# Splitting the products of a weight block around the arrival of its residue (hybrid encoder with PEER, one core)

## The chip, the cores and the metric

One core of one Trainium2 chip. The metric is the device time of one execution in microseconds (us). The kernel before took 3535.6 us, the median of three runs (3535.57 to 3549.32).

## What is computed

Two layers (DEPTH 2) over 512 tokens of width 1024, all in float32:

```python
for l in range(DEPTH):
    h = x @ w_in[l]                                  # 1024 x IN_WIDTH
    ...                                              # three groups of attention heads -> mix
    x = layer_norm(DEEPNORM_ALPHA * x + mix, ln1_g[l], ln1_b[l])
    ffn = peer_ffn(x, peer_w_q[l], peer_sub_keys[l], peer_u[l], peer_v[l])
    x = layer_norm(DEEPNORM_ALPHA * x + ffn, ln2_g[l], ln2_b[l])

def chunk(xc):                                       # in peer_ffn, 128 tokens
    q = (xc @ w_q).reshape(c, PEER_HEADS, 2, PEER_HALF_DIM)
    sc = jnp.einsum('chpd,hpnd->chpn', q, sub_keys)
    top_s, top_i = lax.top_k(sc, kk)                 # 16 of 128, two halves
    ...                                              # 16 of the 256 sums -> experts, gates
    ue = jnp.take(u, experts, axis=0)
    ve = jnp.take(v, experts, axis=0)
    act = jax.nn.gelu(jnp.einsum('chkd,cd->chk', ue, xc), approximate=False)
    return jnp.einsum('chk,chkd->cd', gates * act, ve)
```

The change concerns `xc @ w_q` (the query stage) and the products of x with the experts' rows u (the U stage).

## The kernel before, in words

**Products in three parts.** TensorE works on values rounded to its own 32-bit format (F32R). To keep float32 accuracy an operand is split into a cast part ("hi") and a residue ("lo", the original less the cast), and a product is the sum of three: hi x hi, hi x lo, lo x hi. `product()` (L1449) issues these three, on L1451, L1452 and L1453. The tokens' operand t_hi, t_lo is made once per use, in eight chunks of 128 rows: ScalarE casts (`round_chunks`), VectorE subtracts (`rest_chunks`, L994), and TensorE waits chunk by chunk in `split_chunk` (L1471) where an operand is used for the first time.

**Blocks of weights.** After the attention each layer goes through ST_PER = 16 + 128 + 128 blocks of weights, 128 x 1024 values (512 KB) each: 16 query blocks, 128 U blocks (128 experts each), 128 V blocks. A block goes through a ring of two slots s = 0, 1:

- SyncE loads it into st_raw (`st_load`, L378, the DMA on L381), once the residue of the block two before it, in the same slot, is done (it waits on st_l[s]);
- ScalarE casts it to st_hi (`round_block`, L853, L857), once it has landed and TensorE has finished the block two before it (st_used); it then raises st_h;
- GpSimd computes the residue st_lo = st_raw - st_hi (`rest_block`, L605, L608), and raises st_l[s];
- TensorE runs `stationary()` (L1631): it waits on st_l[s], and then runs, for each of 8 chunks c, the three products of L1451 to L1453 into one PSUM bank, 24 in all, 512 columns wide in the query stage and 384 (tokens 128 to 511) in the U stage. The last one raises st_used.

**Query stage.** `query_pair()` (L1650) runs two blocks and then two sets of four products with the sub-keys; ScalarE copies the queries and the scores out (L875, L880). The first block of the first pair waits for t_lo chunk by chunk. Its residue is made by VectorE (L1000), the others by GpSimd.

**U stage.** `experts()` (L1660) waits until the gelu of the block two before it has emptied its PSUM bank and calls `stationary()`. On ScalarE the order is written out by hand: gelu of block b (L887, into h_out, which SyncE stores on L397), then the cast of block b + 2; before each pair an activation table is loaded. The first 88 U blocks (PRE = 44 pairs) run with nothing between them on TensorE. The other 40 lie between one-hot products of the gates (`spread`, L1684), a stage called B here, which needs the gates of all tokens first: an Exp on ScalarE, a few steps on VectorE (L1317 to L1321), then transposes on TensorE (L1674).

**Beside the 88 blocks.** The first 128 tokens take another way, by gathered rows. VectorE walks 24 units of the top-16 search (`unit`, L1207) in 12 rounds of two, and in each round 8 dot products of x with gathered rows of u (L1292, 512 KB each). A round ends with the eight dots stored (L1305). GpSimd issues the gathers (`gather_rows`, L617, L619) in the same queue in which it computes the residues, in an order written out by hand (`zone`, L635): eight gathers at first, six residues, then six zones of about two rounds, 12 residues and 16 gathers each. A gather waits until VectorE has used the slot's previous row.

**V stage.** Values are weighted and summed with `gather()`, which waits for the cast part and for the residue at separate points already.

Of the kernel before, what the change touches and what calls it, by code (L numbers as in the profile page):

```python
# [37 lines left out]
DC = D // P  # L38
# [31 lines left out]
ST_PER = QB + 2 * EB  # L70
# [63 lines left out]
def build(nc, a, out):  # L134
# [18 lines left out]
    t_hi = keep.tile("t_hi", [P, DC, T], F32R)  # L153
    t_lo = keep.tile("t_lo", [P, DC, T], F32R)
# [73 lines left out]
    st_hi = pr.tile("st_hi", [P, 2, DC, P], F32R)  # L228
    st_lo = pr.tile("st_lo", [P, 2, DC, P], F32R)
# [58 lines left out]
    def sem(name):  # L288
        return ctx.enter_context(nc.semaphore(name))
# [31 lines left out]
    st_h, st_used = sem("st_h"), sem("st_used")  # L321
    st_l = [sem(f"st_l{s}") for s in range(2)]
# [1116 lines left out]
    def _(pe):  # L1439
# [9 lines left out]
        def product(dst, lhs, rhs, first, last):  # L1449

            nc.tensor.matmul(dst, lhs[0], rhs[0], start=first, stop=False)  # L1451
            nc.tensor.matmul(dst, lhs[0], rhs[1], start=False, stop=False)  # L1452
            return nc.tensor.matmul(dst, lhs[1], rhs[0], start=False, stop=last)  # L1453

        with pe.Fori(0, L) as l:
# [15 lines left out]
            def split_chunk(u, c):  # L1471

                pe.wait_ge(tr_lo, DC * (3 * l + u) + c + 1)
# [31 lines left out]
            for k in range(3):  # L1505
                for tb in range(TB):
                    last = nc.tensor.transpose(ps[:, k, tb * P:(tb + 1) * P], lat_n[:, tb, k * P:(k + 1) * P], ident[:])
# [5 lines left out]
            for tb in range(TB):  # L1513
                bank = 4 * ((tb + 1) % 2)
                rows = slice(tb * P, (tb + 1) * P)
# [5 lines left out]
                for half in range(2):  # L1521
                    for k in range(2):
                        last = nc.tensor.matmul(ps[:, bank + half, 0:w], lat_t[:, k, rows],
                                                w_uq[:, k, half * w:(half + 1) * w], start=k == 0, stop=k == 1)
                last.then_inc(lat_ps, 1)
                w = UKV_W // 2
                for half in range(2):
                    last = nc.tensor.matmul(ps[:, bank + 2 + half, 0:w], lat_t[:, 2, rows],
                                            w_ukv[:, half * w:(half + 1) * w], start=True, stop=True)
# [100 lines left out]

            def stationary(m, s, dst, rows, operand=None):  # L1631

                pe.wait_ge(st_l[s], ST_PER // 2 * l + m + 1 + 1)
                for c in range(DC):
                    if operand is not None:
                        split_chunk(operand, c)
                    last = product(dst, (st_hi[:, s, c], st_lo[:, s, c]), (t_hi[:, c, rows], t_lo[:, c, rows]), c == 0,
                                   c == DC - 1)
                last.then_inc(st_used, 1)

            def key_scores(f, s):
# [8 lines left out]
            def query_pair(i, operand=None):  # L1650
                for s in range(2):
                    stationary(i, s, ps[:, s], slice(0, T), operand if s == 0 else None)
                for s in range(2):
                    key_scores(2 * i + s, s)
# [5 lines left out]
            def experts(m, s):  # L1660

                pe.wait_ge(gelu_done, EB * l + 2 * m + s + 1)
                stationary(m + QB // 2, s, ps[:, s, 0:TN], slice(P, T))
# [7 lines left out]
            for k in range(3):  # L1671
                src = e_all[:].rearrange("p u k -> p (u k)") if k == 2 else i_all[:, k]
                for d in range(DB):
                    last = nc.tensor.transpose(ps[:, SEL_BANKS[k], d * P:(d + 1) * P], src[:, (d + 1) * P:(d + 2) * P], ident[:])  # L1674
# [126 lines left out]
```

## Time and profile before

| what | value |
|---|---|
| median of three runs | 3535.6 us (3535.57 to 3549.32) |
| the profiled execution, its own time | 3530.59 us |
| its span, first to last instruction | 3529.0 us |
| TensorE products busy | 3294.9 us (93%) |
| TensorE weight loads busy | 2961.4 us (84%) |
| VectorE busy | 2491.6 us (71%) |
| ScalarE busy | 1367.2 us (39%) |
| GpSimd busy | 1956.2 us (55%) |
| mean granted TensorE clock | 0.977 of full speed |
| bytes moved | 765.11 MB, mean 217 GB/s |

The two layers look alike. In the first, attention runs to about 380 us, the query stage from 393 to 504, the first 88 U blocks to about 938, stage B to 1215, the V stage to 1760.

How to read the rows below. PE is TensorE's products, PEld its weight loads, DVE VectorE, ACT ScalarE, POOL GpSimd, SPq SyncE's queue of DMA issues. A product's shown duration includes its way through the array, so that consecutive ones overlap; the distance between starts of weight loads tells their pace. "<-" behind a time in brackets names what ended the idle time before the instruction, and that time is the number ahead of it.

### The profile page before, as it was taken

The numbers are of one execution on the slowest core, as the hardware profiler recorded it, in microseconds if no ns is written. First come the engines' busy times: TensorE is split into PE (matmuls) and PEld (weight loads), VectorE is DVE, ScalarE is ACT, GpSimd is POOL, SyncE is SP. The second block draws the span as 40 slices with busy tenths as digits, with TensorE's granted clock in tenths as the row PEclk, the third lists the DMA queues.
The fourth block names the chain that finished last, engine by engine and source line by source line (L and its number), as shares of the span: only waits on it lengthen the run. The fifth ranks groups of instructions, "written<-read, shape, count | busy, mean of one in ns | idle before, by whom it ended". The sixth has DMA issues, their size and how long they took to land.

```text
span 3529.0 us, 67255 instructions
## 1 busy us (share of the span) xinstructions
PE 3294.9 (93%) x18452; PEld 2961.4 (84%) x18454; DVE 2491.6 (71%) x5419; ACT 1367.2 (39%) x2110; POOL 1956.2 (55%) x1558
## 2 busy tenths in 40 slices
PE   8999898889999899999899998989899998999996
PEld 8888788888999788888688887888889988888885
DVE  1454554888787688898924545458887877889898
ACT  2354244444433333333324542444444333333332
POOL 3434346777654266666544342467776543666664
PEclk9999999999999999999999999999999999999998
DMA  4001137888788599999820011378887985999996
GB/s 159 25 1 60 48 103 230 285 283 287 248 257 260 161 335 323 338 339 337 306 86 25 1 60 54 111 233 287 282 284 248 270 251 169 347 337 337 339 336 231
DMA packets 402485, 765.11 MB, mean 217 GB/s; under 512 B 162400, under 2 KB 261472, under 8 KB 398432
## 3 DMA queue, kind: packets, MB, share of 16 engines
q1 hardware_dynamic: 197088, 462.06, 39.0%
q0 software_dynamic: 73728, 268.47, 20.8%
q10 hardware_dynamic: 131584, 33.56, 4.5%
q8 instruction: 40, 0.66, 0.1%
q14 instruction: 45, 0.37, 0.0%
HBM read 677.98 MB, written 85.98 MB: 216 GB/s over the span
## 4 chain that ended last, share of the span: by engine, by line
PE 55%; issue 21%; POOL 11%; DVE 5%; DMA 3%; ACTq 3%; ACT 1%; POOLq 1%; DVEq 1%; SPq 0%
PE ps L1717 24%; POOL st_lo L608 6%; PE ps L1451 6%; PE ps L1452 6%; PE ps L1453 6%; PE ps L1684 4%; PE ps L1573 3%; POOL u_row L619 3%; PE ps L1550 3%; ACTq L934 2%; PE ps L1558 2%; DMA h_in<-gelu_d 2%; PE ps L1539 1%; DMA st_raw<-in_peer_v 1%; DMA u_row<-in_peer_ur,idx_u 1%
## 5 line engine op out<-in xcount | busy, mean ns | idle before, releaser
L608 POOL TENSOR_TENSOR st_lo<-st_raw,st_hi 128x1024 fp32r<-128x1024 f32 x290 | 695.5, 2399 | 632.2 <-ACT st_hi L857 628.7
L1451 PE MATMUL ps<-t_hi,st_hi 128*128 128x384 f32 (+1 forms) x2304 | 822.5, 357 | 83.7 <-POOL st_lo L608 80.3
L857 ACT CAST st_hi<-st_raw 128x1024 fp32r<-128x1024 f32 x544 | 570.4, 1048 | 747.6 <-PE ps L1717 462.6
L1453 PE MATMUL ps<-t_hi,st_lo 128*128 128x384 f32 (+1 forms) x2304 | 801.3, 348 | 0.0
L1452 PE MATMUL ps<-t_lo,st_hi 128*128 128x384 f32 (+1 forms) x2304 | 801.2, 348 | 0.0
L717 POOL TENSOR_TENSOR wt_lo<-w_f,wt_hi 128x384 fp32r<-128x384 f32 x256 | 420.4, 1642 | 312.5 <-ACT wt_hi L959 311.1
L1451 PEld LDWEIGHTS ps<-t_hi,st_hi 128*128 128x128 f32 x2304 | 440.3, 191 | 130.7 <-POOL st_lo L608 96.1
L1452 PEld LDWEIGHTS ps<-t_lo,st_hi 128*128 128x128 f32 x2304 | 440.6, 191 | 10.5
L1453 PEld LDWEIGHTS ps<-t_hi,st_lo 128*128 128x128 f32 x2304 | 439.5, 191 | 11.4
L1717 PE MATMUL ps<-st_hi,wt_hi 128*128 128x512 f32 x1536 | 390.4, 389 | 5.3 <-ACT wt_hi L959 5.3
L1717 PE MATMUL ps<-st_lo,wt_hi 128*128 128x512 f32 x1536 | 389.8, 389 | 0.0
L1717 PE MATMUL ps<-st_hi,wt_lo 128*128 128x512 f32 x1536 | 389.7, 389 | 0.0
L887 ACT ACTIVATE h_out<-ps 128x384 f32<-128x384 f32 x256 | 126.0, 492 | 634.6 <-PE ps L1453 601.7
L1387 DVE TENSOR_TENSOR st_lo<-st_raw,st_hi 128x1024 fp32r<-128x1024 f32 x252 | 313.4, 1244 | 72.1 <-ACT st_hi L857 71.6
L1717 PEld LDWEIGHTS ps<-st_hi,wt_hi 128*128 128x128 f32 x1536 | 288.0, 188 | 67.1 <-ACT st_hi L857 4.4
L1717 PEld LDWEIGHTS ps<-st_lo,wt_hi 128*128 128x128 f32 x1536 | 288.4, 188 | 59.9
L1717 PEld LDWEIGHTS ps<-st_hi,wt_lo 128*128 128x128 f32 x1536 | 288.4, 188 | 59.8
L1292 DVE CUSTOM_DVE_ANT_0 u_row<-ps,u_row 128x1024 f32<-128x1024 f32 x192 | 232.8, 1212 | 149.4 <-DMA u_row<-in_peer_ur,idx_u 145.3
L1396 DVE SCALAR_TENSOR_TENSOR ps<-v_row,w_sp,ps 128x1024 f32<-128x1024 f32 x256 | 327.1, 1278 | 1.0
L1379 DVE TENSOR_TENSOR w_f<-g_in,h_in 128x256 f32<-128x256 f32 x256 | 256.0, 1000 | 60.9 <-DMA h_in<-gelu_d 49.1
L619 POOL DMA_INDIRECT v_row<-in_peer_v,idx_v x256 | 255.6, 998 | 43.8 <-issue 17.5
L1343 DVE TENSOR_SCALAR oh<-ps,i_t,g_t 128x128 f32<-128x128 f32 x768 | 260.9, 402 | 0.0
(194 smaller groups left out, 5102.6 us busy)
## 6 DMA issues: line engine op xcount, KB each, us to landing
st_raw<-in_peer_u SPq DMA_DIRECT2D x256, 512.0 KB
st_raw<-in_peer_v SPq DMA_DIRECT2D x256, 512.0 KB
gelu_d<-h_out SPq DMA_DIRECT2D x256, 192.0 KB
h_in<-gelu_d SPq DMA_DIRECT2D x256, 192.0 KB
gates_d<-g_stage ACTq DMA_DIRECT2D x32, 1024.0 KB
g_in<-gates_d SPq DMA_DIRECT2D x256, 128.0 KB
w_raw<-in_w_in SPq DMA_DIRECT2D x16, 1168.0 KB, 5.4
st_raw<-in_peer_w_q SPq DMA_DIRECT2D x32, 512.0 KB
```

The costliest lines, as they stand in the source:

```text
L608: nc.gpsimd.tensor_tensor(st_lo[:, s].rearrange("p c f -> p (c f)"), st_raw[:, s], st_hi[:, s].rearrange("p c f -> p (c f)").bitcast(F32), ...
L619: nc.gpsimd.indirect_dma_start(out=dst, out_offset=None, in_=table, in_offset=bass.IndirectOffsetOnAxis(ap=number, axis=0)).then_inc(lande ...
L717: nc.gpsimd.tensor_tensor(wt_lo[:, s], w_f[:, s], wt_hi[:, s].bitcast(F32), ALU.subtract).then_inc(wt_l, 1)
L857: nc.scalar.copy(st_hi[:, s].rearrange("p c f -> p (c f)"), st_raw[:, s]).then_inc(st_h, 1)
L1343: last = nc.vector.tensor_scalar(oh_1[:, GRP * r + k], iota_ps, i_t[:, 0, ds(t0 + k, 1)], g_t[:, ds(t0 + k, 1)], ALU.is_equal, ALU.mult)
L1379: nc.vector.tensor_tensor(w_f[:, s, 0:T_D], g_in[:, s], h_in[:, s, 0:T_D], ALU.mult)
L1387: nc.vector.tensor_tensor(st_lo[:, s].rearrange("p c f -> p (c f)"), st_raw[:, s], st_hi[:, s].rearrange("p c f -> p (c f)").bitcast(F32), ...
L1396: nc.vector.scalar_tensor_tensor(out=acc, in0=v_row[:, r], scalar=w_sp[:, ds(b, 1)], in1=acc, op0=ALU.mult, op1=ALU.add).then_inc(v_acc, 1)
L1451: nc.tensor.matmul(dst, lhs[0], rhs[0], start=first, stop=False)
L1452: nc.tensor.matmul(dst, lhs[0], rhs[1], start=False, stop=False)
L1453: return nc.tensor.matmul(dst, lhs[1], rhs[0], start=False, stop=last)
L1717: last = nc.tensor.matmul(ps[:, 2 * d + half], w[:, s, d * P:(d + 1) * P], v[:, half * 512:(half + 1) * 512], start=False, stop=True, skip ...
```

## The change

`stationary()` no longer goes through `product()`. It waits for the cast alone (st_h), runs the 16 products that read st_hi, chunk by chunk, then waits for the residue (st_l[s]), and runs the 8 products that read st_lo. The waits of `split_chunk` stay with the first 16. Nothing else is touched.

```diff
             def stationary(m, s, dst, rows, operand=None):
 
-                pe.wait_ge(st_l[s], ST_PER // 2 * l + m + 1 + 1)
+                pe.wait_ge(st_h, ST_PER * l + 2 * m + s + 1)
                 for c in range(DC):
                     if operand is not None:
                         split_chunk(operand, c)
-                    last = product(dst, (st_hi[:, s, c], st_lo[:, s, c]), (t_hi[:, c, rows], t_lo[:, c, rows]), c == 0,
-                                   c == DC - 1)
+                    nc.tensor.matmul(dst, st_hi[:, s, c], t_hi[:, c, rows], start=c == 0, stop=False)
+                    nc.tensor.matmul(dst, st_hi[:, s, c], t_lo[:, c, rows], start=False, stop=False)
+                pe.wait_ge(st_l[s], ST_PER // 2 * l + m + 1 + 1)
+                for c in range(DC):
+                    last = nc.tensor.matmul(dst, st_lo[:, s, c], t_hi[:, c, rows], start=False, stop=c == DC - 1)
                 last.then_inc(st_used, 1)
```

## Rows read from the trace of the kernel before

**Rows 1.** The page's costliest groups: busy us, mean ns, idle before and its releaser

```profile
L1451 PE MATMUL ps<-t_hi,st_hi 128*128 128x384 f32 (+1 forms) x2304 | 822.5, 357 | 83.7 <-POOL st_lo L608 80.3
```

**Rows 2.** Busy us of PE, PEld, DVE, ACT, POOL (count), clock, DMA share, GB/s, by stretch

```profile
440.00:484.00 44.00, 44.00 (x218) 36.58 (x216) 27.78 (x104) 13.57 (x19) 16.69 (x7) 1.00 0.24 81
748.00:792.00 44.00, 39.09 (x206) 37.03 (x205) 37.60 (x122) 19.35 (x27) 33.19 (x22) 0.96 0.87 293
1672.00:1716.00 44.00, 44.00 (x196) 36.45 (x195) 39.29 (x44) 16.12 (x22) 28.16 (x25) 1.00 0.94 337
```

**Rows 3.** Waits from 400 to 920 us (two rows) and from 920 to 1200: total, times, longest

```profile
PEld ps L1451 <- POOL st_lo L608: 47.2, 40, 9.0
ACT st_hi L857 <- DMA st_raw<-in_peer_u: 40.4, 22, 3.4
...
PEld ps L1451 <- POOL st_lo L608: 0.8, 3, 0.3
```

**Rows 4.** Timeline of one stall, 782 to 792 us: start, duration, engine, operation, idle before

```profile
782.96 1.05 ACT L857 CAST st_hi<-st_raw 128x1024 fp32r<-128x1024 f32 x1 [3.15 <-DMA st_raw<-in_peer_u]
784.09 2.34 POOL L608 TENSOR_TENSOR st_lo<-st_raw,st_hi 128x1024 fp32r<-128x1024 f32 x1 [2.83 <-ACT st_hi L857]
...
786.49 0.29 PEld L1451 LDWEIGHTS ps<-t_hi,st_hi 128*128 128x128 f32 x1 [3.29 <-POOL st_lo L608]
786.58 0.95 POOL L619 DMA_INDIRECT u_row<-in_peer_ur,idx_u  x1
...
789.74 0.19 PEld L1453 LDWEIGHTS ps<-t_hi,st_lo 128*128 128x128 f32 x1
...
791.67 0.19 PEld L1452 LDWEIGHTS ps<-t_lo,st_hi 128*128 128x128 f32 x1
```

**Rows 5.** Timeline: issues of loads on SyncE's queue, and casts

```profile
774.82 0.33 SPq L381 DMA_DIRECT2D st_raw<-in_peer_u  x1
...
786.66 0.33 SPq L381 DMA_DIRECT2D st_raw<-in_peer_u  x1
...
792.93 1.04 ACT L857 CAST st_hi<-st_raw 128x1024 fp32r<-128x1024 f32 x1
...
796.69 0.33 SPq L381 DMA_DIRECT2D st_raw<-in_peer_u  x1
...
801.56 1.04 ACT L857 CAST st_hi<-st_raw 128x1024 fp32r<-128x1024 f32 x1
```

**Rows 6.** DMA issues: count, KB each, median us from issue to landing

```profile
w_raw<-in_w_in SPq DMA_DIRECT2D x16, 1168.0 KB, 5.4
...
x_tok<-in_x SPq DMA_DIRECT2D x1, 2048.0 KB, 7.5
```

**Rows 7.** Timeline of GpSimd: the residues at both ends of one zone

```profile
743.63 2.42 POOL L608 TENSOR_TENSOR st_lo<-st_raw,st_hi 128x1024 fp32r<-128x1024 f32 x1
...
803.43 2.42 POOL L608 TENSOR_TENSOR st_lo<-st_raw,st_hi 128x1024 fp32r<-128x1024 f32 x1
```

**Rows 8.** Timeline: residues behind the first eight gathers, and the next cast

```profile
564.76 4.68 POOL L608 TENSOR_TENSOR st_lo<-st_raw,st_hi 128x1024 fp32r<-128x1024 f32 x2
...
574.00 1.04 ACT L857 CAST st_hi<-st_raw 128x1024 fp32r<-128x1024 f32 x1
```

**Rows 9.** Timeline of VectorE: the sum of the gates behind ScalarE's Exp

```profile
937.56 0.69 DVE L1317 TENSOR_REDUCE z_all<-e_all 128x32 f32<-128x512 f32 x1 [7.34 <-ACT e_all L909]
```

**Rows 10.** Timeline: the eight chunks of t_lo, and the second query block's first load

```profile
392.00 4.88 DVE L994 TENSOR_TENSOR t_lo<-ps,t_hi 128x512 fp32r<-128x512 f32 x8 [2.96 <-ACT t_hi L762]
...
398.86 0.19 PEld L1451 LDWEIGHTS ps<-t_hi,st_hi 128*128 128x128 f32 x1 [0.70 <-POOL st_lo L608]
```

**Rows 11.** Timeline of VectorE: ends of three rounds

```profile
657.53 0.16 DVE L1305 TENSOR_TENSOR dots<-dot,ps 128x8 f32 x1 [0.43 <-DVE i_all L1265]
...
685.91 0.16 DVE L1305 TENSOR_TENSOR dots<-dot,ps 128x8 f32 x1 [0.43 <-DVE i_all L1265]
...
928.07 0.16 DVE L1305 TENSOR_TENSOR dots<-dot,ps 128x8 f32 x1 [0.43 <-DVE i_all L1265]
```

## The prediction, made before the changed kernel ran

> **What bounds the kernel now.** I read the page first: which engine is busiest, and what TensorE waits for. The chosen line is the first product of a block, L1451. TensorE sat idle 83.7 us before it, 80.3 of them until GpSimd's residue st_lo was there (L608) [rows 1]. That is the wait the change addresses, in two layers together.
>
> The second view is the busy time by stretches [rows 2]. In the query stage TensorE is busy 44.0 of 44 us: there is nothing to gain. In the U stage it is busy 39.1 of 44, at a granted clock of 0.96, with the DMA engines at 0.87 and 293 GB/s. In the V stage, which the diff does not touch (gather() already waits in parts), it is full again.
>
> The third view is the waits of one stretch each [rows 3]. From 400 to 920 us the weight loads wait 47.2 us for st_lo. In the same stretch ScalarE waits 40.4 us, 22 times, for the 512 KB load of st_raw, which no order of products makes earlier. After 920 us, where one-hot products lie between the blocks, the wait for st_lo is 0.8 us: no gain there. So everything lies in one stage per layer, some 370 us long.
>
> The timeline of one long stall shows the mechanism [rows 4]. The cast is at 782.96 (1.05 us, so done by 784.01), the residue at 784.09 (2.34), and TensorE, idle since 783.2, starts at 786.49, 3.29 idle. It then finds its clock halved: ten steps take 3.25 us until 789.74 (1.2 GHz), 0.325 each, and the eleven after them 1.93 us, 0.175 each (2.4 GHz). I counted six such slow stretches in this stage of the first layer, most behind a stall of 3 us or more; this one stands for them. A block of 24 is 4.2 us at the full clock; its 16 cast-only products are 2.8, the last 8 are 1.4.
>
> **The change, part by part.**
>
> *The instructions.* No product, load or store is added or removed; 24 products stay 24. One semaphore wait is added per block, 144 blocks per layer (16 query, 128 U). Where it is already met I price it at nothing: blocks follow each other with a wait between them in the full query stage [rows 2]. What covers it is the queue of products already issued. Its upper bound is one product's step, 0.175 us, per wait, were nothing queued: 0.175 x 288 = 50 us, which I leave out of the range, since that price would show as idle time between the blocks of the query stage, and there is none. What is queued behind the new wait on TensorE is the last 8 products, then the next block or the one-hots, and ScalarE (gelu, then the cast two blocks on) waits for the last of them. None of these is served later than before: the block used to end 4.2 us after the residue at the earliest, now it can end 1.4 us after it.
>
> *What is late next.* ScalarE casts block n+2 after gelu of block n, and st_raw for n+2 is loaded once the residue of block n is done. So a two-slot ring remains without TensorE in it: load, cast 1.05, residue 2.4, load again. Where a cast came 4.87 us after its load's issue (796.69 to 801.56 [rows 5]) it was TensorE that held it: 0.1 for the start, 4.2 for the block, 0.5 for the gelu. Those casts can come earlier, down to the load's own time. The trace shows that time only where the cast waited for it: 8.14 us (774.82 to 782.96), with gathers in flight [rows 4, 5]. From below I take the landings of undisturbed loads: 5.4 us for 1168 KB and 7.5 for 2048 KB [rows 6], a slope of 2.1 us per 880 KB, so 3.8 us for 512 KB. Between 3.8 and 4.87 I take 4.3, the middle, as both rows are equally near.
> The Trainium skill (DMA: Bandwidth & Descriptors, section Anatomy of one DMA) fits 2.0 us plus the bytes at 436 GB/s; an estimate by it is 3.2 us for 512 KB, by which the zones below would gain about a third more again. Its fit is for GpSimd's queue, and no run here shows that time.
>
> *One zone.* GpSimd's order is fixed: 12 residues and 16 gathers (0.95 us each for GpSimd, and up to 0.3 of gap [rows 4]) make a zone, and six zones make most of the stage. The one between the residues at 743.63 and 803.43 takes 59.8 us [rows 7]. I walked it through in the new order, measured load times where the cast waited, 4.3 where it did not: each load issued 0.1 after a residue's end, each residue after its cast and after the gather ahead of it. The first six blocks bring 0.7 us. The loads of 8.14 and its neighbour hold as before, so the residue of 784.09 comes 0.8 earlier. The next cast was held by TensorE: its load is issued at 786.66, TensorE's block ends at 792.5 because of stall and slow clock, the cast is at 792.93 [rows 5]. In the new order the block's 16 products run from 784.0 beside the residue, it ends near 788, and the load decides: with 5.5 us (between 3.8 and 6.27) the cast comes about 1.6 earlier. The zone ends 1.4 us earlier. With every load at 3.8 it would be 3.6, then with GpSimd's own order as the bound; with every load as late as its cast it would be nothing. Six zones: 8.4 us, between 0 and 22.
>
> *The start of the stage.* GpSimd issues eight gathers in a row and makes two residues late, at 564.76 (4.68 us for both); the next cast is at 574.00 [rows 8]. With the new order the first of the two blocks needs only its last 8 products after 567.1, so it ends near 569 instead of 573, and the cast is held by its load (issued 567.35) to about 571.8. The blocks after it come 3.0 to 4.2 earlier; I take 3.7, bounds 2.2 and 4.2.
>
> *The end of the stage.* The last blocks would end 3.9 earlier (2.8 from the overlap, the rest from a slow stretch at 915 to 919). But ScalarE's Exp of the gates stands behind one more cast, whose load is issued after a residue, and VectorE waits 7.3 us for that Exp now [rows 9]. By that queue 2.3 us is left, bounds 0 and 3.9.
>
> *The first query block.* It takes t_lo chunk by chunk, and 8 chunks need 4.88 us, 0.61 each [rows 10]. Three products per chunk (0.70) covered that pace; two (0.46) do not, and 8 products of 0.23 are left at the end: the block ends 1.0 us later. The second block, which now waits 0.70 for its residue until 398.86 [rows 10], no longer does. Net loss 0.35, bounds 1.0 and a gain of 0.3.
>
> **The sum.** 8.4 + 3.7 + 2.3 - 0.35 = 14.05 us per layer, 28 for two. The bounds are 2 us (0 + 2.2 + 0 - 1.0, twice) and 60 (22 + 4.2 + 3.9 + 0.3, twice). The profiled execution took 3530.6 us, so it would be 3502.6; the median of the three runs shown, 3535.6, stands 5.0 above it, and the forecast against that is 3507.6.
>
> **A ceiling.** VectorE walks its 12 rounds in the same stage, 28.38 us a round when nothing holds it (657.53 to 685.91). The eight rounds from there to 928.07 took 242.2 against 227.0 [rows 11]. So these alone can shrink by 15 us, plus the 7.3 of the Exp, before VectorE decides: no limit to the forecast (8.4 for all twelve rounds), a cap on anything far larger.
>
> **The rivals.**
> (A) *The transfers absorb it.* The DMA engines are at 0.87 in this stage, and the V stage shows 0.94 and 337 GB/s at best [rows 2]. If loads issued earlier only take longer beside the gathers, the zones give 0 to 0.5 each, and start and end remain: 4 to 17 us in all, 3519 to 3531. For it: 22 casts already wait for loads. Against: in 50 of 72 blocks of the zones the cast was not waiting for one. That the early wait is met no earlier than the late one, so that the change does nothing, belongs here; the 2.4 us between cast and residue in every block speak against it.
> (B) *The loads are short.* At 3.8 us, and with the six slow-clock episodes per layer gone, 42 to 66 us: 3470 to 3493. Against it: GpSimd's order takes over, and crowding lengthens loads.
> (C) *Slower, through TensorE's clock.* A stall of 3.3 us halved the clock for ten products, 0.15 us lost on each, 1.5 us per episode [rows 4]. If splitting a block makes the engine idle twice per block and the clock falls more often, each new episode costs that. It takes 28 / 1.5 = 19 more episodes to eat the forecast and 31 to be 0.5% slower, against 12 now: 3553 or above. For it: two places to wait instead of one. Against: the total idle falls, and each single stall gets shorter.
> The Trainium skill (TensorE: Matmul & The Clock Gate, section HAM oscillation) says that waits between bursts of products drop the clock again and again; by that rule the split is a risk where both parts wait. The trace agrees that a long stall does it.
>
> **How the numbers follow.** Forecast 0.58 (18 to 42 us gained, 3494 to 3518), A 0.21, B 0.15, C 0.06. About 0.5% (18 us) is what a measurement can tell here. Faster by more: 0.58 + 0.15 and a little of A, 0.75. Within: 0.19. Slower: 0.06. The range of 3473 to 3527 leaves out C, the weakest part of A and the end of B.
>
> **What would show it.** Right: the wait for st_lo moves from L1451 to the first of the last 8 products and falls from 83.7 us to under 30; casts wait more for st_raw (over 77.6 us in all); the query stretch stays at 44.0; fewer than six slow stretches per layer; the U stage from first gather to last round some 12 us shorter, the B and V stages as long as before. Wrong: if the casts' wait for loads grows as much as TensorE's falls and the rounds still take 30 us (A), or if the granted clock in the U stage falls below 0.96 (C).

## The result and the profile after

Six runs of the changed kernel on the chip took 3507.95 us in the median (3504.69 to 3517.27), six of the kernel before 3535.59 (3530.37 to 3549.32). The ratio is 0.9917, with a 95% interval of 0.9899 to 0.9934. The profiled execution took 3504.7 us, its span 3503.1 against 3529.0 before. The forecast was 3507.6.

The page of the changed kernel, costliest groups (busy us, mean ns, idle time before them and its releaser); L1637 is now the first product of a block, L1641 the first of the eight that read the residue:

```profile
L1637 PE MATMUL ps<-t_hi,st_hi 128*128 128x384 f32 (+1 forms) x2304 | 820.9, 356 | 50.6 <-ACT st_hi L857 49.1
...
L1641 PE MATMUL ps<-t_hi,st_lo 128*128 128x384 f32 (+1 forms) x2304 | 471.5, 347 | 12.1 <-POOL st_lo L608 11.9
```

Against the 83.7 us of [rows 1]: the wait for the residue is nearly gone (12.1), but 50.6 us of a new one stand ahead of the block, for the cast. TensorE's idle time at the blocks went from 83.7 to 62.7 us, 21 less, in a span that is 26 less. (L1641's busy time is shorter because its eight products now follow each other: they overlap, and the page counts the overlap once.) What holds the cast stands in the waits of the changed kernel, 400 to 920 us (total, times, longest), beside [rows 3]:

```profile
ACT st_hi L857 <- DMA st_raw<-in_peer_u: 105.6, 56, 5.9
...
PEld ps L1637 <- ACT st_hi L857: 29.8, 16, 3.8
...
PEld ps L1641 <- POOL st_lo L608: 7.0, 3, 6.4
```

Casts waited for their load 22 times and 40.4 us before, now 56 times and 105.6. Over the whole execution the casts' wait for U loads grew from 77.6 to 217.6 us. TensorE left the ring of load, cast and residue, and what is late now is the load. The same three stretches as in [rows 2] (busy us of PE, PEld, DVE, ACT, POOL, clock, DMA share, GB/s):

```profile
440.00:484.00 44.00, 44.00 (x214) 36.46 (x213) 28.84 (x107) 14.00 (x20) 16.79 (x7) 1.00 0.24 80
748.00:792.00 44.00, 41.98 (x236) 41.65 (x236) 39.27 (x124) 21.24 (x29) 34.60 (x26) 0.99 0.88 294
1672.00:1716.00 44.00, 44.00 (x196) 36.44 (x195) 38.07 (x44) 15.54 (x22) 29.76 (x26) 1.00 0.93 333
```

The query and V stages are as full as before; only the U stage changed, 42.0 us busy where it was 39.1. That stretch flatters the change: over the whole of the first layer's U stage the busy share went from 333.5 of 375 us to 333.3 of 364, and the granted clock from 0.96 to 0.95 (in the second layer from 0.96 to 0.97). Now the stage piece by piece. Copies of gather numbers on GpSimd mark its rounds; the sum of the gates on VectorE marks its end. First the kernel before, then the changed one:

```profile
553.71 0.19 POOL L625 COPY idx_u<-idx 128x8 uint32<-128x8 uint32 x1
590.18 0.19 POOL L625 COPY idx_u<-idx 128x8 uint32<-128x8 uint32 x1
889.99 0.20 POOL L625 COPY idx_u<-idx 128x8 uint32 x1
```

```profile
553.91 0.19 POOL L625 COPY idx_u<-idx 128x8 uint32<-128x8 uint32 x1
587.55 0.19 POOL L625 COPY idx_u<-idx 128x8 uint32<-128x8 uint32 x1
880.00 0.20 POOL L625 COPY idx_u<-idx 128x8 uint32 x1
...
924.41 0.69 DVE L1317 TENSOR_REDUCE z_all<-e_all 128x32 f32<-128x512 f32 x1 [5.90 <-ACT e_all L909]
```

In the first layer the start of the stage took 36.47 us and takes 33.64, 2.8 less. Five zones took 299.8 and take 292.5: 7.4 less, 1.5 per zone. From there to the gates, which holds the sixth zone and the end, 47.57 (937.56 in [rows 9]) became 44.41, 3.2 less. That is 13.35 us in the first layer; between the same marks the second went from 382.60 to 367.38, 15.2 less: 2.7 at the start, 10.0 in the five zones (2.0 each), 2.5 at the end. Together 28.6. Each is one profiled execution of a stage that varies: with the old order in the U stage, `query_only` below took 296.7 and 304.9 us for the same five zones in its two layers, and `u_only`, with the new one, 292.3 and 289.3. The mean of four layers is 300.2 for the old order and 290.9 for the new, 1.9 us per zone.

The start shows what a split block does and what it does not (weight loads, a residue pair, and the cast held by its load):

```profile
560.79 0.19 PEld L1638 LDWEIGHTS ps<-t_lo,st_hi 128*128 128x128 f32 x1
564.95 4.70 POOL L608 TENSOR_TENSOR st_lo<-st_raw,st_hi 128x1024 fp32r<-128x1024 f32 x2
567.37 2.42 PEld L1641 LDWEIGHTS ps<-t_hi,st_lo 128*128 128x128 f32 x8 [6.39 <-POOL st_lo L608]
569.78 0.33 PEld L1637 LDWEIGHTS ps<-t_hi,st_hi 128*128 128x128 f32 x1
...
572.51 1.05 ACT L857 CAST st_hi<-st_raw 128x1024 fp32r<-128x1024 f32 x1 [1.54 <-DMA st_raw<-in_peer_u]
```

The last of the block's 16 cast-only products starts at 561.0, beside the gathers. Then TensorE waits 6.39 us in the middle of the block, comes back at half its clock (a weight load of 0.33 us instead of 0.19), and the last eight products take 2.42 us instead of 1.4. The next cast comes at 572.5 instead of 574.0 [rows 8]; it waited for its load, 4.96 us from the issue at 567.55.

### The profile page after: what moved, and what is told of

The parts are those of the page before. It is cut to its first block, busy times and chain, and to the rows that moved or that the text cites. A ratio compares the mean times of both kernels' runs of the same rounds, so it can differ in the third digit from the quotient of the medians.

```text
span 3503.1 us, 67417 instructions
## 1 busy us (share of the span) xinstructions
PE 3287.7 (94%) x18454; PEld 2970.9 (85%) x18454; DVE 2484.8 (71%) x5419; ACT 1370.6 (39%) x2110; POOL 1955.3 (56%) x1558
## 4 chain that ended last, share of the span: by engine, by line
PE 52%; issue 21%; POOL 12%; DMA 6%; DVE 3%; ACTq 3%; ACT 1%; POOLq 1%; DVEq 1%; SPq 0%
PE ps L1720 22%; POOL st_lo L608 7%; PE ps L1687 4%; DMA h_in<-gelu_d 4%; POOL u_row L619 4%; PE ps L1573 3%; PE ps L1451 3%; PE ps L1452 3%; PE ps L1453 3%; PE ps L1550 3%; PE ps L1637 3%; PE ps L1638 3%; PE ps L1641 3%; ACTq L934 2%; PE ps L1558 2%
## 5 line engine op out<-in xcount | busy, mean ns | idle before, releaser
L1637 PE MATMUL ps<-t_hi,st_hi 128*128 128x384 f32 (+1 forms) x2304 | 820.9, 356 | 50.6 <-ACT st_hi L857 49.1
L1637 PEld LDWEIGHTS ps<-t_hi,st_hi 128*128 128x128 f32 x2304 | 444.4, 193 | 76.1 <-ACT st_hi L857 59.9
L1641 PE MATMUL ps<-t_hi,st_lo 128*128 128x384 f32 (+1 forms) x2304 | 471.5, 347 | 12.1 <-POOL st_lo L608 11.9
L1641 PEld LDWEIGHTS ps<-t_hi,st_lo 128*128 128x128 f32 x2304 | 415.0, 190 | 26.8 <-POOL st_lo L608 15.2
L1292 DVE CUSTOM_DVE_ANT_0 u_row<-ps,u_row 128x1024 f32<-128x1024 f32 x192 | 232.5, 1211 | 123.4 <-DMA u_row<-in_peer_ur,idx_u 74.3
```

The costliest lines, as they stand in the source:

```text
L1637: nc.tensor.matmul(dst, st_hi[:, s, c], t_hi[:, c, rows], start=c == 0, stop=False)
L1641: last = nc.tensor.matmul(dst, st_lo[:, s, c], t_hi[:, c, rows], start=False, stop=c == DC - 1)
```

## The experiments

The kernel before ran on the same chip beside each set of runs, and each ratio stands against that. The theory: the stage goes by a ring of two slots (load, cast, residue, load), TensorE's block was a link in it and is out of it now. The rivals: TensorE, GpSimd's order, VectorE, or the rate of the DMA engines as the bound.

**Where the gain is: one stage at a time.** The split in the U blocks alone (`u_only`):

```diff
             def stationary(m, s, dst, rows, operand=None):
 
+                if dst.shape[-1] == TN:
                     pe.wait_ge(st_h, ST_PER * l + 2 * m + s + 1)
...
+                else:
+                    pe.wait_ge(st_l[s], ST_PER // 2 * l + m + 1 + 1)
...
```

A U block is TN = 384 columns wide, a query block 512.

> Only the U blocks are split; the query blocks keep the old order. Theory (the gain is all in the first 88 U blocks of each layer, and the query stage pays a little in its first block): the same gain as the whole change, 28 us, perhaps 0.5 us more (ratio 0.991 to 0.993). Rival (part of the gain comes from the query stage, by queries that are ready sooner): 2 us or more of the gain is missing.

Measured: 3508.3 us, ratio 0.9921 (0.9897 to 0.9945). That is 25 us; no part of the gain is missing within the interval.

The opposite condition (`query_only`):

```diff
-                if dst.shape[-1] == TN:
+                if dst.shape[-1] != TN:
```

> Only the 16 query blocks are split. Theory: no gain, a loss of 0.5 us in two layers, not to be told from none (3535); in the trace the first query block takes about 0.3 us longer, 6.4 from its first product to the next block's first instead of 6.1, since two products per chunk do not cover the 0.6 us that a chunk of t_lo takes. Rival: 2 us or more faster.

Measured: 3536.9 us, ratio 1.0019 (1.0001 to 1.0038): no gain, and a loss that the interval puts between 0.4 and 13 us. The trace sizes what the query stage itself loses, and shows the mechanism. The first query block of the changed kernel (weight loads):

```profile
393.54 0.19 PEld L1637 LDWEIGHTS ps<-t_hi,st_hi 128*128 128x128 f32 x1 [0.88 <-DVE t_lo L994]
...
394.14 0.19 PEld L1637 LDWEIGHTS ps<-t_hi,st_hi 128*128 128x128 f32 x1 [0.30 <-DVE t_lo L994]
...
397.72 0.19 PEld L1637 LDWEIGHTS ps<-t_hi,st_hi 128*128 128x128 f32 x1 [0.30 <-DVE t_lo L994]
...
399.92 0.19 PEld L1637 LDWEIGHTS ps<-t_hi,st_hi 128*128 128x128 f32 x1
```

The first product of each of the seven later chunks waits 0.30 us for t_lo. The block lasts 6.38 us to the next one's first product; before it was 6.12, from 392.74 to 398.86 [rows 10]. In `query_only` it is 6.37 (393.21 to 399.58). So the first block costs 0.26 us. The whole query stage, from its first product to the first U product, takes 105.1 us in both layers of the kernel before and of `u_only`, and 105.5 to 105.6 in those of the changed kernel and of `query_only`: 0.4 us per layer.

**How much must be moved.** Half of the cast-only products ahead of the wait (`eight_first`):

```diff
-                for c in range(DC):
+                for c in range(DC // 2):
...
                 pe.wait_ge(st_l[s], ST_PER // 2 * l + m + 1 + 1)
+                for c in range(DC // 2, DC):
...
+                    nc.tensor.matmul(dst, st_hi[:, s, c], t_hi[:, c, rows], start=False, stop=False)
+                    nc.tensor.matmul(dst, st_hi[:, s, c], t_lo[:, c, rows], start=False, stop=False)
```

> Of the 16 products that need only the cast, 8 run ahead of the wait for the residue and 8 behind it, so a block can end 2.8 us after its residue instead of 1.4 (and 4.2 before). Theory (casts are held by their loads once TensorE is out of their way, and the load needs 4 to 4.5 us while gelu and cast follow TensorE by 0.6): half the move gives most of the gain, since 2.8 + 0.7 is already below the load's time; start and end of the stage lose about 1.4 us each per layer; 18 to 24 us faster than before. Rival (the gain is in proportion to the products moved): 14 us.

Measured: 3510.5 us, ratio 0.9936 (0.9910 to 0.9961), 23 us below the kernel before. It is what the theory gave, but the interval is 9 us to either side and just reaches the rival's 14. The waits say more: from 400 to 920 us the casts waited for their load 55 times, where the kernel before has 22 and the full split 56. So half the move already leaves the load as what comes last. The weight loads still waited 33.8 us, 40 times, for the residue (47.2 and 40 before), and 16.3 for the cast.

**Longer blocks.** Two more products per U block, 0.35 us, behind the residue, into a free bank, in both kernels (`before_plus2`, `after_plus2`):

```diff
                 pe.wait_ge(st_l[s], ST_PER // 2 * l + m + 1 + 1)
+                if more:
+                    pe.wait_ge(sc_ev, QB * (l + 1) + PRIME)
+                    for c in range(2):
+                        nc.tensor.matmul(ps[:, 2, 0:TN], st_hi[:, s, c], t_hi[:, c, rows], start=True, stop=True)
```

> The kernel before with two more products of 384 columns (0.35 us) behind the residue in each of the first 88 U blocks, into a free PSUM bank: 31 us of TensorE per layer. Theory (TensorE's block is a link of the ring load, cast, residue, block, cast in most blocks): 35 to 55 us slower than before in two layers. Rival (TensorE is beside the ring): under 15 us.

> The changed kernel with the same two products. Theory (TensorE is out of the ring, the casts wait for loads): at most 25 us slower than the changed kernel, clearly less than in the kernel before; the rest is taken by idle time. Rival (TensorE is still a link in most blocks): 35 us or more, as in the kernel before.

Measured: 3552.5 us (ratio 1.0066, 1.0040 to 1.0092) in the kernel before, and 3517.7 (0.9957, 0.9936 to 0.9978) in the changed one. So 62 us more of TensorE's work cost 23 us in the old order and about 14 in the new one (0.9957 against the 0.9917 of the changed kernel, measured beside other runs; the two intervals leave the 0.4% open to 0.1 or 0.7). The second is what I had expected, at most 25; the first is less, 23 where I had put 35 to 55. The likely reading is that TensorE was the last link in fewer blocks than the casts' waits suggest. That the new order feels the products less is likely too, not shown.

**Shorter loads.** U loads from the fifth block on move half of their columns, in both kernels (`before_half`, `after_half`). The other half of each block's load is left out; all instructions stay:

```diff
-                    st_load(i + QB // 2 + 2, s, a["peer_u"][l, 2 * i + 4 + s])
+                    half_load(i + QB // 2 + 2, s, a["peer_u"][l, 2 * i + 4 + s])
...
+                sp.dma_start(st_raw[:, s, 0:DC * P // 2], src[:, 0:DC * P // 2]).then_inc(s_straw[s], 16)
```

> The kernel before, with the loads of U blocks 4 and up moving only the first half of their columns (256 KB instead of 512; the other half is left out, stale data is used). Theory (before the change most casts were held by TensorE, not by their load): a gain of 10 to 25 us, from the 22 load-held casts per layer alone. Rival (the DMA engines' rate was the bound already): 50 us or more.

> The changed kernel with the same halved loads (the other half left out). Theory (after the change the casts are held by their loads): the halved load gives more here than in the kernel before, 25 to 45 us below the changed kernel (3465 to 3485), then VectorE's rounds of 28.4 us or GpSimd's order hold the stage. Rival (GpSimd's order or VectorE holds it already): under 8 us below the changed kernel.

Measured: 3480.0 us (0.9860, 0.9834 to 0.9886) in the old order, 3474.9 (0.9843, 0.9817 to 0.9869) in the new one. Here my expectation for the old order fell: 51 us instead of 10 to 25. Its rival, the rate of the DMA engines as the bound, named 50 or more; the runs with halves below move all the bytes and tell the two apart. With short loads the old order is nearly as good as the new: 5 us apart. VectorE's rounds in `before_half` say what holds the stage then:

```profile
653.00 0.16 DVE L1310 TENSOR_TENSOR dots<-dot,ps 128x8 f32 x1 [0.43 <-DVE i_all L1270]
681.37 0.16 DVE L1310 TENSOR_TENSOR dots<-dot,ps 128x8 f32 x1 [0.43 <-DVE i_all L1270]
709.73 0.16 DVE L1310 TENSOR_TENSOR dots<-dot,ps 128x8 f32 x1 [0.43 <-DVE i_all L1270]
```

28.37 and 28.36 us, the 28.38 of [rows 11]: the ceiling named in the prediction is reached, in both orders. In `before_half` the casts' wait for loads from 400 to 920 us is down to 0.8 us, once. So the loads are the root, and the split is a way to lose less by them: TensorE has 16 products to run while the residue behind a late load is made. Without late loads the zones go by VectorE in both orders, and 5 us is all that the split gives. The edit shortens every load, the short ones too, so it does not say how much of the 51 us the long ones alone cost.

The changed kernel's own loads show how long they are (issue on SyncE's queue, then the cast that waited for it; the second pair is twice as far apart):

```profile
777.51 0.33 SPq L381 DMA_DIRECT2D st_raw<-in_peer_u  x1
...
781.38 1.05 ACT L857 CAST st_hi<-st_raw 128x1024 fp32r<-128x1024 f32 x1 [1.38 <-DMA st_raw<-in_peer_u]
```

```profile
769.22 0.33 SPq L381 DMA_DIRECT2D st_raw<-in_peer_u  x1
...
776.92 1.05 ACT L857 CAST st_hi<-st_raw 128x1024 fp32r<-128x1024 f32 x1 [1.75 <-DMA st_raw<-in_peer_u]
```

3.87 and 7.70 us for the same 512 KB.

**A shorter ring: the residue and the load in halves.** A load needs the residue of the slot's last block. With the residue in two halves the first half of the load can go 1.2 us sooner, half of a residue of 2.35 us (`halves`, and the same edit in the old order, `before_halves`). The loads are halved for the first 88 U blocks, from the fifth on; the cast waits for both halves. The residue is made in halves for every block that GpSimd serves:

```diff
+            def load_halves(m, s, src):
+
+                sp.wait_ge(st_p[s], (ST_PER - EB) // 2 * l + m + s * (l + 1) - 1)
+                sp.dma_start(st_raw[:, s, 0:DC * P // 2], src[:, 0:DC * P // 2]).then_inc(s_half[s], 16)
+                sp.wait_ge(st_l[s], ST_PER // 2 * l + m + 1)
+                sp.dma_start(st_raw[:, s, DC * P // 2:], src[:, DC * P // 2:]).then_inc(s_straw[s], 16)
...
-                nc.gpsimd.tensor_tensor(st_lo[:, s].rearrange("p c f -> p (c f)"), st_raw[:, s],
-                                        st_hi[:, s].rearrange("p c f -> p (c f)").bitcast(F32),
-                                        ALU.subtract).then_inc(st_l[s], 1)
+                for part in range(2):
+                    at_c = slice(part * DC // 2, (part + 1) * DC // 2)
+                    at_f = slice(part * DC * P // 2, (part + 1) * DC * P // 2)
+                    nc.gpsimd.tensor_tensor(st_lo[:, s, at_c].rearrange("p c f -> p (c f)"), st_raw[:, s, at_f],
+                                            st_hi[:, s, at_c].rearrange("p c f -> p (c f)").bitcast(F32),
+                                            ALU.subtract).then_inc((st_p, st_l)[part][s], 1)
```

> The changed kernel, and the residue on GpSimd in two halves of 512 columns; the load of the next block into the slot goes in two halves too (first 88 U blocks), the first one issued when the first half is subtracted, 1.2 us sooner. Theory (the ring of load, cast and residue is the bound): the loads land 0.5 to 1 us sooner, and 5 to 15 us are gained over the changed kernel. Rival (GpSimd's own order is the bound): two instructions of overhead more per block make it 5 to 15 us slower than the changed kernel. Rival (the DMA engines' rate is the bound): no change.

> The kernel before with the residue and the load in two halves, and the old order of products. Theory (a long load holds the ring, and the split lets TensorE run beside it; both shorten the same ring, whose floor is VectorE's rounds of 28.4 us, which the run with halved loads reached from either order): most of the halves' 25 us is there without the split, and the split is worth 5 to 20 us on top (this one at 3490 to 3505). Rival (the two are independent): 3508, 25 us above the run with both.

Measured: 3483.2 us with the split (0.9854, 0.9828 to 0.9881) and 3491.2 without (0.9878, 0.9853 to 0.9904). The halves alone gain 42 us, more than the split alone (28), and more than the 5 to 15 us that I had expected of them. The split adds 8 us on top by the medians, which the two intervals leave open to nothing; the traces do show it, from the first U product to the gates 417.9 and 417.8 us without the split, 410.8 and 409.4 with it. Both are faster than the changed kernel, `halves` by 25 us. The casts' wait for loads in `before_halves`, 400 to 920 us, where it was 40.4 us:

```profile
ACT st_hi L877 <- DMA st_raw<-in_peer_u: 5.1, 9, 1.2
```

The rounds of `halves`:

```profile
651.37 0.16 DVE L1325 TENSOR_TENSOR dots<-dot,ps 128x8 f32 x1 [0.43 <-DVE i_all L1285]
679.74 0.16 DVE L1325 TENSOR_TENSOR dots<-dot,ps 128x8 f32 x1 [0.43 <-DVE i_all L1285]
708.10 0.16 DVE L1325 TENSOR_TENSOR dots<-dot,ps 128x8 f32 x1 [0.43 <-DVE i_all L1285]
```

VectorE's floor again, with whole loads this time. The rival of GpSimd's order is out: it runs more instructions here and the kernel is faster. So is the rate of the DMA engines: all bytes move in less time. Whether the earlier start helps or the smaller size of each transfer, no run tells apart.

**Below VectorE's floor?** VectorE stands idle at the start of the stage, 48.4 us ahead of its first dot product on L1292 in the kernel before:

```profile
560.33 1.23 DVE L1292 CUSTOM_DVE_ANT_0 u_row<-ps,u_row 128x1024 f32<-128x1024 f32 x1 [48.36 <-DMA u_row<-in_peer_ur,idx_u]
```

Two constants of GpSimd's order let the first gathers go after 2 U blocks instead of 14, with 14 residues per zone instead of 12: in the old order, the new one, and with the halves (`before_early`, `after_early`, `halves_early`):

```diff
-ZONE_R, ZONE_B0, ZONE_BN = 2, 14, 12
+ZONE_R, ZONE_B0, ZONE_BN = 2, 2, 14
```

> The kernel before with other constants of GpSimd's order: the first eight gathers go out after 2 U blocks instead of 14, and each zone has 14 residues instead of 12 for its 16 gathers. Theory (the loads are long where gathers run beside them, and VectorE stands idle 48 us per layer at the start of the stage): rounds of 7 blocks leave 17% more time per gather, loads are shorter, 10 to 40 us faster than before. Rival (only the TensorE, cast, residue chain counts): no change, the eight gathers cost the same stall earlier.

> The same constants in the changed kernel. Theory: VectorE no longer holds the stage, its rounds end before the blocks do; the stage goes by TensorE and the loads, 10 to 40 us below the changed kernel. The split is still worth 10 us or more against the run of the same constants in the old order; if loads were short everywhere it would be worth only the end and the start, some 8 us.

> All three: the split, the halves and the constants. Theory: with VectorE's floor gone and the loads short, TensorE is nearly full in the stage, 4.3 us a block: 20 to 40 us below the halves run (3445 to 3465). Rival (GpSimd's order, or the loads again): within 10 us of it.

Measured: 3544.2 us (1.0034, 1.0012 to 1.0056), 3542.7 (1.0012, 0.9990 to 1.0034) and 3481.9 (0.9855, 0.9826 to 0.9883). Every theory here missed; of the rivals only the last one's number came out, within 10 us of `halves`. VectorE's rounds in `before_early`:

```profile
657.67 0.16 DVE L1305 TENSOR_TENSOR dots<-dot,ps 128x8 f32 x1 [0.42 <-DVE i_all L1265]
693.20 0.16 DVE L1305 TENSOR_TENSOR dots<-dot,ps 128x8 f32 x1 [0.42 <-DVE i_all L1265]
```

35.5 us for seven blocks; over the first layer's five zones it is 344.9 us for 70 blocks, 4.9 a block. In the kernel before it is 299.8 for 60, 5.0 a block. Fewer gathers per block made the blocks hardly faster, and twelve more of them, which ran at 4.3 us without gathers, now have gathers beside them. So my idea that the stage gets shorter with more time per gather is wrong, and how a load and the gathers beside it come to 7 or 8 us stays open.

The pair also bounds what the split is worth: 1.5 us, where I had expected 10 or more, and the two intervals leave it open to nothing. The five zones take 344.9 and 338.3 us in `before_early`, 344.8 and 340.3 in `after_early`; only start and end are shorter, by 6.2 and 3.8 us a layer together. So the split's gain in the zones hangs on GpSimd's order, and why it is gone under this one no run shows.

## Why the prediction was right, step by step

*The place.* All of it is in the first 88 U blocks: the two runs with one stage each show that.

*The zones.* Predicted 1.4 us per zone, measured 1.5 in the first layer, 2.0 in the second, 1.9 in the mean of four layers of each order. The undisturbed load was taken as 4.3 us between 3.8 and 4.87; the shortest that held a cast in the changed kernel took 3.7 to 4.0, the lower end. The landings in the traces (from the issue to the last of the load's 16 semaphore steps, where all 16 were recorded) say how the loads went in the U stages: a median of 4.2 us and 25 of 125 over 6 us before, 4.3 and 25 of 112 after. So the price of 4.3 was fair for a load in the middle, and rival A's condition, loads that get longer because they start earlier, is hardly seen. One zone was walked through and six priced by it; where two layers of one kernel differ by up to 8 us in five zones, that it came so near is in part luck.

*The start.* Predicted 3.7, measured 2.8 and 2.7. Two things were missed. The first cast, at 572.51 where the term had 571.8, was held by its load, which took 4.96 us where I had allowed 4.45. The next one was held by TensorE at its lower clock: the wait in the middle of the block is still 6.4 us, the eight products behind it take 2.42 us, and the next block begins slow at 569.78 and hands over at 574.87, 5.1 us for a block of 4.2.

*The end.* Predicted 2.3 and 1.4 for the sixth zone, 3.7; measured 3.2 and 2.5, with VectorE waiting 5.9 us for the Exp instead of 7.3.

*The first query block.* Predicted 0.35 lost per layer, measured 0.26 at that block and 0.4 over the query stage.

*The sum.* 14.05 per layer predicted; 12.9 and 14.8 measured, which is 13.35 and 15.2 less 0.4 each. That the forecast and the median differ by less than a microsecond is luck: the measurement is good to some 6 us.

*The added wait.* Priced at nothing, and the query stretch is at 44.0 of 44 as before. Of the 0.4 us that the query stage lost, 0.26 are the first block's; what is left for the other 15 blocks is about 0.01 us each. Shown.

*The signs.* The wait for st_lo moved to L1641 and fell to 12.1 us, under the 30 that were named. From the first gather to the last round the stage is 11.1 and 14.2 us shorter, where some 12 were named, and the stages behind it are as long as before within 2 us. The first half of the sign for rival A came too: the casts' wait for loads grew by 140 us, TensorE's idle time fell by 21. It was no sign of A, since a cast that no longer waits for TensorE shows the load as its releaser; the rounds, 30.1 us in the mean of nine before and 29.2 after, decide.

*What was wrong.* A small miscount first: the 3.25 us of [rows 4] are eleven steps, not ten. Then three readings. First, "fewer than six slow stretches per layer": the first layer has eight, the second five, and in both together 154 weight loads took over 0.25 us instead of 134; 20 more at 0.15 us each are 3 us. The clock over the first layer's stage is 0.95, below the 0.96 that was named for rival C. What the sign for the residue did not see is the new idle time ahead of the block, 50.6 us for the cast. Rival C's mechanism was there, an order too small. The Trainium skill (TensorE: Matmul & The Clock Gate, section HAM oscillation) says waits between bursts bring this; the trace agrees. Second, against rival A I held that 50 of 72 casts did not wait for a load. The runs with halved loads and with the halves refute the use of that count: shorter or earlier loads gain 42 to 51 us in the old order. A late load delays the casts behind it through TensorE, and those then show TensorE as their releaser, as in [rows 4, 5]: the cast of 792.93 stands behind the late load of 782.96. Third, I took TensorE for the link in most blocks; lengthening its blocks by 62 us in all cost 23.

*The ceiling* by VectorE was right: the rounds of 28.4 us hold the stage in four of the runs, both with halved loads and both with halves.

## What to carry to other kernels

Where a product needs two parts that become ready one after the other, run all of it that needs the first part, then wait: it cost 0.4 us per layer in the query stage, and gave 25 to 28 us where the second part was late. The gain is no constant of the pattern: it was 5 to 8 us once the loads were shorter or earlier, and about none under another order of gathers and residues. But ask first what makes the part late. A ring with few slots is best shortened at its root, here by freeing the load's buffer in halves (42 us), and the count of who released whom does not find that root, because one late transfer shows up as several waits for others. Leaving out half of the suspected transfer, with every instruction kept, pointed to it, and a run that moved all the bytes sooner confirmed it.

## What the runs showed of the hardware

From its issue to the cast that waited for it, a 512 KB load took 3.7 to 8.4 us in the U stages of the changed kernel: 55 of 115 up to 4.9, 26 up to 6.4, 34 above. The mean rate there was 294 GB/s in one stretch, where the V stage moves 333. The mean rate says little about one transfer. The Trainium skill (DMA: Bandwidth & Descriptors, section Anatomy of one DMA) gives 2.0 us plus the bytes at 436 GB/s, an estimate of 3.2 us here by its fit for GpSimd's queue. The shortest of these, 3.7 us with the cast's own start in it, stands 0.5 above that. In the query stage of the kernel before, without gathers beside them, 512 KB loads landed 3.1 to 3.6 us after their issue, and there the trace agrees; the 3.8 us that the prediction took for an undisturbed load was high.

A stall in the middle of a block drops TensorE's clock as one between blocks does: eight products in 2.42 us behind a wait of 6.39, where eight take 1.4.
